# Attention heads of a long and a short query tile in turn, with two groups of heads open at once

## The reference

```python
# A: top-k keys of an indexer, one key/value head shared by all query heads
logits = einsum('bqhd,bqkd->bqhk', qb, kg) * scale        # masked to the selected keys
out    = einsum('bqhk,bqkd->bqhd', softmax(logits), vg)
# B: causal, with a decay from the cumulated log forget values
logits = einsum('bqhd,bkhd->bhqk', qb, k) * scale + decay  # masked to earlier keys
out    = einsum('bhqk,bkhd->bqhd', softmax(logits), v)
```

## Time and profile before

| | us |
|---|---|
| three runs | 2593.61, 2594.66, 2659.35 |
| median | 2594.66 |
| profiled execution | 2590.64 |
| its span | 2588.8 |
| attention stage, layer 0 (423.24 to 542.30) | 119.06 |
| attention stage, layer 1 (1488.98 to 1608.60) | 119.62 |
| mean granted TensorE clock, whole span | 0.916 |

### The profile page before, as it was taken

How to read it: one execution, slowest core, us unless ns; L and a number is a source line. 1 busy time by engine, 2 the same in 40 slices (tenths; PEclk the granted TensorE clock), 3 DMA queues, 4 the chain that set the end, 5 groups by cost and what they waited for, 6 DMA issues and landing times.

```text
span 2588.8 us, 44970 instructions
## 1 busy us (share of the span) xinstructions
PE 2440.5 (94%) x17364; PEld 2286.4 (88%) x17364; DVE 1409.6 (54%) x2604; ACT 939.3 (36%) x1805; POOL 469.4 (18%) x327
## 2 busy tenths in 40 slices
PE   7998998999699999989899899988999999999997
PEld 5998996679699999989799866877999999999997
DVE  4587814543566576423193353432676666667665
ACT  2324312302321122142432132133665665655554
POOL 1333420003000000013334000200330231231230
PEclk8999998879699999989999896985999999999997
DMA  6344210012354454212222000203554554555552
GB/s 242 114 138 139 82 66 13 1 53 89 131 158 148 142 171 141 74 58 70 82 94 87 17 13 13 74 18 116 180 208 163 188 195 169 186 180 180 176 179 89
DMA packets 54183, 300.01 MB, mean 116 GB/s; under 512 B 6502, under 2 KB 6992, under 8 KB 34864
## 3 DMA queue, kind: packets, MB, share of 16 engines
q1 hardware_dynamic: 51632, 290.39, 32.8%
q0 software_dynamic: 2432, 7.94, 1.0%
HBM read 291.81 MB, written 6.49 MB: 115 GB/s over the span
## 4 chain that ended last, share of the span: by engine, by line
PE 54%; issue 37%; DVE 4%; POOL 2%; ACT 2%; DMA 2%; POOLq 0%; SPq 0%; ACTq 0%; DVEq 0%
PE ps L1142 22%; PE ps L832 9%; PE ps L771 6%; PE ps L1122 3%; PE ps L1181 3%; PE ps L722 2%; POOL slotsR L626 2%; PE ps L992 2%; PE ps L976 1%; PE ps L702 1%; DMA pp<-in_ada_w 1%; PE ps L952 1%; DVE gT L1628 1%; PE ps L1100 1%; PE ps L1126 1%
## 5 line engine op out<-in xcount | busy, mean ns | idle before, releaser
L1205 PE MATMUL ps<-hR,wR 128*128 128x272 f32 x2112 | 277.5, 296 | 22.8 <-DVE wR L2060 22.8
L1205 PEld LDWEIGHTS ps<-hR,wR 128*128 128x128 f32 x2112 | 276.4, 195 | 23.1 <-issue 23.1
L832 PE MATMUL ps<-hH,slotsR 128*128 128x272 f32 x1536 | 293.0, 290 | 3.9 <-ACT oT L1359 3.9
L626 POOL TENSOR_TENSOR slotsR<-slots,slotsR 128x1024 fp32r<-128x1024 f32 x64 | 155.8, 2455 | 664.5 <-ACT slotsR L1310 664.5
L832 PEld LDWEIGHTS ps<-hH,slotsR 128*128 128x128 f32 x1536 | 244.3, 190 | 4.5 <-issue 4.5
L1142 PE MATMUL ps<-hg,wR 128*128 128x320 f32 (+1 forms) x1536 | 223.1, 307 | 4.9 <-DVE wR L1984 4.9
L1142 PEld LDWEIGHTS ps<-hg,wR 128*128 128x128 f32 x1536 | 219.7, 205 | 5.3 <-DVE wR L1984 5.3
L832 PE MATMUL ps<-hL,slotsR 128*128 128x272 f32 x768 | 223.5, 291 | 0.0
L626 POOL TENSOR_TENSOR slotsR<-slots,wz 128x1000 fp32r<-128x1000 f32 x36 | 92.6, 2595 | 713.4 <-ACT wz L1310 713.4
L771 PE MATMUL ps<-wz,hH 128*128 128x250 f32 (+1 forms) x720 | 206.9, 287 | 13.8 <-POOL slotsR L626 7.2
L771 PE MATMUL ps<-slotsR,hH 128*128 128x250 f32 (+1 forms) x720 | 205.5, 285 | 0.0
(11 more groups left out here) (324 smaller groups left out, 5079.1 us busy)
## 6 DMA issues: line engine op xcount, KB each, us to landing
slots<-in_moe_gu_w SPq DMA_DIRECT2D x90, 1024.0 KB, 4.9
pp<-in_ada_w SPq DMA_DIRECT2D x88, 512.0 KB, 4.2
slots<-in_moe_down_w SPq DMA_DIRECT2D x64, 704.0 KB, 4.0
slots<-in_gate_w SPq DMA_DIRECT2D x24, 1024.0 KB, 4.9
slots<-in_ffn_gu_w SPq DMA_DIRECT2D x22, 1024.0 KB, 7.2
slots<-in_z_w SPq DMA_DIRECT2D x18, 1000.0 KB, 4.9
slots<-in_ffn_down_w SPq DMA_DIRECT2D x16, 704.0 KB, 5.6
slots<-in_out_w SPq DMA_DIRECT2D x8, 1024.0 KB, 4.8
```

The costliest lines, as they stand in the source:

```text
L626: G.tensor_tensor(low_part[:, c], raw[:, c], high[:, c].bitcast(FP), ALU.subtract).then_inc(pw_split, 1)
L832: last = mm(ps[:, 2 * out_pair + a, 0:HALF], w[:, c], r[:, n], start=(k == i == 0), stop=(k == KD - 1 and i == 2))
L1205: last = mm(ps[:, 2 * out_pair + h, 0:HALF], wR[:, buf, a, k * P:(k + 1) * P], rhs(k, b)[:, c], start=(first and k == 0 and i == 0), stop= ...
```

## The change

The list of items is built from five pairs of groups; in a pair, a head of one group alternates with a head of the other. A group's number is now `group(j)`: even for the first of a pair, odd for the second, so the two open groups use the two banks and the two sets of row sums. `group_end` says whether an item is the last head of its group, and `turned` names the group whose rows are turned back at an item: the even group `lag` items after its last head, the odd one `lag` + 1 items after. TensorE's loop runs one item further and ScalarE's seven, for the last two groups. Nothing else in the kernel is touched; the two waits for group g-2 stay as they are, with the new numbers.

```diff
-        items = [(t, m, h) for t in (3, 2, 1, SAMPLE, 0) for m in range(2) for h in range(AH)]
+        pairs = (((3, 0), (0, 0)), ((3, 1), (0, 1)), ((2, 0), (SAMPLE, 0)), ((2, 1), (SAMPLE, 1)), ((1, 0), (1, 1)))
+        items = [(t, m, h) for pair_of in pairs for h in range(AH) for t, m in pair_of]
+
+        def group(j):
+
+            return 2 * (j // (2 * AH)) + j % 2
+
+        def group_end(j):
+
+            return 0 <= j < NATT and items[j][2] == AH - 1
+
+        def turned(i, lag):
+
+            return [j for j in (i - lag, i - lag - 1) if group_end(j) and group(j) % 2 == i - lag - j]
...
# TensorE: values, and turning back
-                    tm = j // AH
+                    tm = group(j)
...
-                for i in range(NATT + 5):
+                for i in range(NATT + 6):
...
-                    j = i - 4
-                    if 0 <= j < NATT and j % AH == AH - 1:
+                    for j in turned(i, 4):
...
# ScalarE
-                for i in range(NATT):
+                for i in range(NATT + 7):
+                    if i >= NATT:
+                        for j in turned(i, 5):
+                            ot_copy(j)
+                        continue
...
-                    tm = i // AH
+                    tm = group(i)
...
-                    if i >= 5 and (i - 5) % AH == AH - 1:
-                        ot_copy(i - 5)
-                ot_copy(NATT - 1)
+                    for j in turned(i, 5):
+                        ot_copy(j)
...
# VectorE
-                    if 0 <= j < NATT and j % AH == AH - 1:
+                    if group_end(j):
                         t, m, h = items[j]
-                        r, tm = ROWS[t], j // AH
+                        r, tm = ROWS[t], group(j)
```

## The result

The changed kernel takes 2722.68 us, the median of four executions from 2721.8 to 2734.06, against a median of 2594.14 for the kernel before: 1.0531 times as long, 95% interval 1.0508 to 1.0554. Ratios and intervals here leave out executions that ran over 1.5% longer than the fastest of the same kernel, for the kernel before the one of 2659.35 us, so a ratio is not the quotient of two medians. The forecast was slower, 2697 in a range of 2645 to 2735. The profiled execution has a span of 2720.0 us and a mean granted clock of 0.872, against 2588.8 and 0.916.

What follows compares the result with a forecast made beforehand. Matmul time and TensorE's clock were taken to set the attention stage. Lead-in, pair groups, boundaries and drain summed to 170.0 us a layer against 119.06, +51, two layers +102 on the median 2594.66: 2697, range 2645 to 2735.

Steps and rivals of the forecast that it cites:

- first rival: Clock falls before the boundary, in the attention stage's first pairs: +17 us a layer, 2714 to 2731; chance 0.12.
- the fall at the first boundary: Forecast: attention clock falls to 0.50 some 25 to 31 us in and stays; +51 us a layer; chance 0.56.
- The row that the prediction held against such a fall: The attention stage's first stretch: TensorE busy 2.46 of 4.00 us, yet clock 1.00.
- a chain of 4.3 us with 1.9 idle: At a pair boundary at 2.4 GHz, closing groups takes 4.3 us; TensorE idles about 1.9, at least 1.3.
- the 0.5 assumed: Cost in us of each pair boundary at 1.2 GHz, where doubled work covers the chain; three boundaries 1.5.
- The sum of layer 1: Attention stage of a layer, summed from lead-in, pair groups, boundaries and drain: 170.0 us against 119.06, +51.
- the deduction for the filling pipeline: First pair group: 3.2 us off 21.6, its first exponentials coming while the pipeline fills, leaving 18.4.
- Half speed: Long attention heads at 1.2 GHz were taken to cost 1.85 times their full-clock time.
- third rival: Clock falls at a later boundary: at the second 2666 us, at the third 2637; chance 0.14.
- Nothing in the stage brings it back: Once fallen at the first boundary, the clock was expected to stay at half speed through the attention stage.
- fourth rival: Clock falls and returns inside the stage, or half speed costs long heads much less than 1.85: 2600 to 2640; chance 0.04.
- second rival: Clock holds through the attention stage, stage near 112 us, -7 a layer, 2578; chance 0.14.

Runs made afterwards that it cites:

- a_bound: The changed kernel with unread matmuls added: four at the stage's start, two and four at each boundary between pair groups; 2665.56 us, ratio 1.0293.
- a_sums4: The changed kernel with four buffers of row sums, so the exponential waits for group g-4 instead of g-2; 2691.14 us, ratio 1.0393.
- b_stall: The kernel before, order unchanged, with twelve chained fills on VectorE ahead of each stage's first row maximum; 2730.58 us.
- a_start: The changed kernel with four unread matmuls ahead of the first transposes of the attention stage; 2702.14 us, ratio 1.0436.
- a_hold: a_bound's added matmuls in the changed kernel, plus one a pair ahead of the long head's values in the first four pair groups; 2655.81 us, ratio 1.0247.
- s_order: The changed kernel with four sets of row sums, four unread matmuls at the start, and other pairs that spread thin groups over denser ones; 2681.71 us, ratio 1.0378.
- b_gap: The kernel before with VectorE held up ahead of the first tile-2 head's maximum, four memsets in layer 0, eight in layer 1; 2637.34 us, ratio 1.0204.
- s_last: The changed kernel with four sets of row sums, four unread matmuls at the start, other pairs, both sample groups paired last; 2580.23 us, ratio 0.9981.
- s_hold: The changed kernel with four sums sets, four start matmuls, three more per pair in groups three and four, one in the last; 2641.99 us, ratio 1.0074.
- b_hold: The kernel before, order unchanged, with one unread matmul ahead of the values of each sample and tile-0 head; 2617.92 us, ratio 1.0104.

## Why the prediction was right

**The verdict and the mechanism.** Slower by over 2% had 0.78, and the clock was named as the cause; a_bound, a_sums4 and b_stall show it from three sides. The number came from the forecast in one layer and from its first rival in the other, and the range held because it had been drawn to take that rival in.

**The fall.** Layer 1 did what was forecast: the fall at the first boundary, 30.6 us into the stage (25 to 31 forecast), half speed to the end. Layer 0 did what the first rival said, at a chance of 0.12, and a_start shows it was the idle time at the stage's start. The row that the prediction held against such a fall, 2.46 of 4.00 busy at clock 1.00, was the old kernel's; by the same cut the changed kernel has 1.77. That the new order thins the start was overlooked. Layer 1 has the same 1.77 and survived; why only layer 0 fell there stays open. By the first rival for one layer the forecast would have been 2697 + 17 = 2714; measured 2722.68.

**The boundary.** Forecast a chain of 4.3 us with 1.9 idle; measured 4.86 and 2.06. The price at full clock is as much: from the first long score of m=1 to the third, across the boundary in layer 1, the changed kernel takes 1589.02 - 1578.53 = 10.49 us and a_sums4 1580.98 - 1572.61 = 8.37, 2.12 less. (The 23.20 and 20.65 of the first groups differ by more, 2.55, since they are cut at an exponential that itself comes earlier without the wait.) At half speed four boundaries together cost (613.58 - 423.18) - (610.60 - 421.63) = 1.4 us (first exponential to end of layer 0's stage, the changed kernel less a_sums4, both at half speed nearly throughout), 0.4 each for the 0.5 assumed, or a little more, since the changed kernel kept its clock 0.9 us longer at the start.

**The sum of layer 1**, 170.0 forecast and 177.01 measured, by the same cuts (each half-speed boundary put to the group before it, the 1.5 us that still ran fast to the second): start 2.0 and 1.93; first group with its boundary 20.3 and 23.20; second 39.2 and 40.40; third 35.3 and 36.74; fourth 36.5 and 39.80; last 31.9 and 27.67; drain 4.8 and 7.27. Two terms were mis-sized. The pairs of the first group were right (3.6 forecast, 3.71), but the deduction for the filling pipeline was not: 18.4 without boundary became 20.65 in a_sums4, a deduction of 1.6 where 3.2 was taken. And the fourth group, tile 2 m=1 with the sample m=1, takes 6.6 us a pair instead of 6.0. The last group and the drain must be taken together, 36.7 forecast and 34.94, since the exponential at the cut between them runs ahead of TensorE.

**Half speed** at 1.85 times for long heads was right: 1.79 to 1.90 in b_stall.

**Behind the boundary** the prediction had no term for what came next, as the fall had come already. With the boundary filled or its wait gone, the clock falls in the third pair group, 11 to 18 us behind its first exponential: later than the third rival's fall at the second boundary, and without an idle boundary to make it. "Nothing in the stage brings it back" held for the changed kernel; in a_bound (layer 1), a_hold (both) and s_order (layer 0) it came back in the last pair group, what the fourth rival, at 0.04, had allowed.

**The second rival**, that the clock holds, was to give -7 us a layer. By the Trainium skill (TensorE: Matmul & The Clock Gate, section "Loop structure matters more than you think") VectorE's copies between matmuls leave the clock alone and long DMA waits take it. But the loop that the page calls good is one whose next matmuls follow immediately, and at a boundary they do not; the prediction left that condition out when it said that by this rule the clock would hold. The runs add that the wait need not be for DMA: the fall in layer 1 came after a boundary on VectorE and ScalarE at a DMA share of 0.02, and b_stall and b_gap dropped the clock with VectorE alone. What the order gives at full clock stays open: s_last's -3.2 and -3.9 us, in another order of pairs, are the most that was seen of the forecast -7, and the one stage of the changed pairs that ran at 1.00 (s_hold) was longer than before, with its extra matmuls.

## What to carry to other kernels

Before an order is changed, ask of the dense stretch what it does to TensorE's pauses, and cost a fall of the clock not at the pause itself but at all that follows until the clock is back: here 1.8 to 1.9 times for dense heads and 1.65 times for a pair of tile 3 with tile 0. Look at the start of a stage as well as at its boundaries: a shorter second item thinned it here. A buffer count that was slack can become the pause when groups begin to end together: four sets of row sums instead of two took it away here. Put thin work where nothing is queued behind it that could be slowed.

## What the runs showed of the hardware that was not expected

Unread matmuls were nearly free where TensorE had gaps: in a_hold against a_bound, twelve more instructions (six matmuls, each in two passes) in the second group made 26.54 into 26.91 us, 0.06 a matmul; in the thin sample heads at half speed (b_hold) six cost 17.49 - 12.66 = 4.8, 0.8 each.

The clock also falls without a pause in the profile. In s_last TensorE is shown busy 4.00 of 4.00 in the stretch of the fall (519.3), in the sample's group:

```profile
517.00:521.00 4.00, 4.00 (x27) 2.41 (x27) 2.05 (x13) 1.80 (x7) 0.00 (x0) 0.79 0.00 0
```

The kernel before did the same at 502. So the busy share that a trace shows for a stretch does not by itself tell whether the stretch keeps its clock.
